# Two diffusion layers on one core: the experts' results go through a table in DRAM, and their weights through 16 fixed homes of half a unit

## The chip, the core and the metric

The kernel runs on one core of a Trainium2 chip. The metric is the device time of one execution in microseconds (us). A core has a matrix engine (TensorE, PE in the rows; PEld is its loading of weights), a vector engine (VectorE, DVE), a scalar engine (ScalarE, ACT), GpSimd (POOL) and SyncE (SP), which here only starts transfers. Each has its own queue of instructions, and they wait for each other by semaphores. 16 DMA engines move data between DRAM and the core's memory.

## The reference, cut to what matters

Two layers over 256 latent tokens of width 1024 with 256 context tokens, all in float32. The even layer mixes attention and a Fourier part and has a dense SwiGLU; the odd layer has a gated short convolution, and then eight experts of which each token uses two:

```
D_MODEL, SEQ, N_EXPERTS, TOP_K, D_EXPERT = 1024, 256, 8, 2, 3584

def swiglu(h, w_gate, w_up, w_down):
    return (jax.nn.silu(h @ w_gate) * (h @ w_up)) @ w_down

def moe_swiglu(h, router, w_gate, w_up, w_down):
    probs = jax.nn.softmax((h @ router).astype(jnp.float32), axis=-1)
    vals, idx = lax.top_k(probs, TOP_K)
    wts = vals / jnp.sum(vals, axis=-1, keepdims=True)
    combine = jnp.sum(jax.nn.one_hot(idx, N_EXPERTS, dtype=jnp.float32) * wts[..., None], axis=-2)
    out = jnp.zeros_like(h)
    for e in range(N_EXPERTS):
        out = out + combine[..., e:e + 1] * swiglu(h, w_gate[e], w_up[e], w_down[e])
    return out

# in reference(), second layer:
    x = x + gt1 * rmsnorm(y_lat, g_post_mix)
    h_lat = modulate(x, g_pre_ch, sh2, sc2)
    y_lat = moe_swiglu(h_lat, o_router[o], o_exp_gate[o], o_exp_up[o], o_exp_down[o])
    x = x + gt2 * rmsnorm(y_lat, g_post_ch)
```

## The kernel before

**Weights.** All large weights come as one stream of units of 128 x 4096 floats (2.1 MB). The first 54 units (`BASE`) belong to everything ahead of the experts; each expert has 21, namely 14 of gate and up columns (`GU_UNITS`) and 7 of down rows. SyncE loads each unit in two halves of 1.05 MB into a ring of 7 units (`RING`), in the order of the stream (line 275). A half is loaded into a slot when TensorE's products with the half that stood there are done: semaphores `first_used` and `used` go one way, `landed` the other. The sum `acc` (128 x 6144) and the gates' rows `gg` are buffers beside the ring. By the time of the experts much of `acc` is free.

**Ahead of the experts** come the modulation products, attention, the dense feed-forward (gate and up products line 1272, down products line 1235, the latter beginning at about 327 us), the convolution (line 1323) and the router. DVE picks two experts for each token, gives each token a slot in the lists of its experts, and chooses for each expert the smallest of seven widths (`WIDTHS`) that holds its list. GpSimd writes the normalized rows to a DRAM buffer (`rows_store`) and the lists to another (`slot_table`).

**An expert.** TensorE has an arm of code for each width and jumps into the arm of the next expert at the end of one (`enter_arm`). Widths 64 and 96 are narrow: the tokens stand still in TensorE and the weights stream (line 1511), 64 slots by two tiles of the array side by side and blocks of 32 slots by four; the products are then turned by transposes (`turn`, line 1470). The others are wide: the weights stand still (line 1486). ACT applies Silu (line 583) and DVE multiplies (line 985). The down products (`down`, line 1553) go into PSUM banks 4 to 7. In this run the eight experts have 64, 96, 144, 64, 128, 64, 96 and 64 slots; that is read from the forms of the instructions.

At the end of an expert the following happens in this order. ACT and DVE copy the down products to `y_slot` (lines 604 and 990), for which they wait on `ye_ps`; where a width has fewer than four parts, a semaphore instruction ahead of the last down unit (line 1532) counts up for the missing ones. TensorE turns the rows of the next expert, which GpSimd has fetched by the token list (line 380) into `xn`: 16 transposes, `turn_expert`, line 1413, after down unit `TURN_AFTER`, the last one. ACT and DVE scale and shift them into `hTe` (lines 558 and 931). Then TensorE multiplies `y_slot` by a weighted selection `selT`, which DVE makes in `weigh`, so that each token's row gets its share (`combine`, line 1583), and DVE adds the result to `y_sum` (line 996). After the last expert follow the norm and the output.

Of the kernel before, what the change touches and what calls it, by code (L numbers as in the profile page):

```python
# [21 lines left out]
P = 128  # L22
# [25 lines left out]
TURN_AFTER = NFE // 4 - 1  # L48
# [41 lines left out]
assert PER_EXPERT % RING == 0 and len(WIDTHS) <= 8  # L90
LAPS = PER_EXPERT // RING
HALF = UNIT // 2

# [12 lines left out]
def build(nc, stream, x_in, ctx_in, vecs, consts, rope, dft, gains, ada_b, norm_w, late, out):  # L106
    ctx = ExitStack()
    with ctx:
# [12 lines left out]
        acc = sb("acc", [P, 6 * D])  # L121
        gg = sb("gg", [P, 2, D])
# [11 lines left out]
        rows_store = nc.dram_tensor("rows_store", (SEQ, D), F32).ap()  # L134
        slot_table = nc.dram_tensor("slot_table", (SEQ * E, 2), F32).ap()
# [35 lines left out]
        y_sum = acc[:, 0:2048].rearrange("p (b d) -> p b d", b=TB)  # L171
        y_slot = acc[:, 2048:4096].rearrange("p (b d) -> p b d", b=2)
        empties = aT[:, 5632:5664]
        sel = acc[:, 4096:4608].rearrange("p (b s) -> p b s", b=TB)
        slot_list = acc[:, 4608:4704].rearrange("p (c w) -> p c w", w=2)
        entry = acc[:, 4704:4712].rearrange("p (b j w) -> p b j w", b=TB, w=2)
        selT = acc[:, 5120:5632].rearrange("p (b t) -> p b t", b=2)
        ramp, before, beats = acc[:, 5632:5889], acc[:, 5889:6017], acc[:, 4720:4848]
        iota, iota1 = ramp[:, 0:SEQ], ramp[:, 1:SEQ + 1]
        duel = acc[:, 2048:2304].rearrange("p (b e h f) -> p b e h f", b=TB, e=E, h=2)  # L180
        router_s = acc[:, 4848:4912].rearrange("p (k e) -> p k e", e=E)
        shift_r = acc[:, 4912:4976].rearrange("p (e k) -> p e k", e=E)
        shift_sum, shift_logit = acc[:, 4976:4984], acc[:, 4984:4992]
        junk = hTe[:, :, :].rearrange("p k t -> p (k t)").rearrange("p (b d) -> p b d", b=TB)

        def small(a, n, w):
            return acc[:, 6024 + a:6024 + a + 2 * n].rearrange("p (b e) -> p b e", b=TB)[:, :, 0:w]
# [6 lines left out]
        first_used = [sem(f"first_used{s}") for s in range(RING)]  # L194
# [29 lines left out]
            sem(n) for n in ("router_ok", "shift_ps", "rows_free", "hTe_wide", "y_sq"))  # L224

# [10 lines left out]


# [31 lines left out]
        def _(sp):  # L269
# [13 lines left out]
            with sp.Fori(1, BASE // RING + 1) as lap:  # L283
                for s in range(RING):
                    sp.wait_ge(used[s], lap)
                    for h in range(2):
                        load(lap * RING + s, s, h)
            lap = BASE // RING + 1
            for s in range(RING):
                if (lap - 1) * RING + s < BASE:  # L290
                    sp.wait_ge(used[s], lap)
                else:
                    sp.wait_ge(first_used[s], 1)
                load(lap * RING + s, s, 0)
# [1438 lines left out]
```

## Time and profile before

| | |
|---|---|
| time, median of 3 runs | 1483.48 us (1483.24 to 1487.16) |
| the profiled execution | 1484.72 us |
| its span in the trace | 1482.8 us |
| TensorE busy | 1432.0 us (97%) |
| VectorE, ScalarE, GpSimd busy | 374.6, 252.4, 42.5 us |
| DMA | 477.09 MB, mean 322 GB/s |

The span runs from the first to the last instruction; the time has some 2 us more. Busy time of TensorE is counted with modelled ends of the matmuls, so that small waits between two can be hidden in it. In the chain of work a piece named "issue" is time in which the engine waited for nothing that the profile shows.

### The profile page before, as it was taken

The page shows a single profiled execution, that of the slowest core. Times are in us where ns is not written, and L with a number is a line of the kernel's source. Part 1 is how long each engine was busy: PE and PEld are TensorE (multiplying, and loading weights), DVE is VectorE, ACT ScalarE, POOL GpSimd, SP SyncE. Part 2 cuts the span into 40 slices and gives each one's busy share as a digit, 9 for nine tenths or more (in the row PEclk, how much of TensorE's full clock was granted, in tenths as well). Part 3 has the DMA queues.
Part 4 walks back from the last instruction along what each step waited for, and adds up shares of the span by engine and source line. Part 5 has one row for each costly group of instructions (what it writes and reads, how often), then busy time and mean ns, then how long its engine had stood idle before and what let it go on. Part 6 is the DMA issues. An engine that isn't in the chain of part 4 may idle for free.

```text
span 1482.8 us, 22551 instructions
## 1 busy us (share of the span) xinstructions
PE 1432.0 (97%) x9386; PEld 921.0 (62%) x9386; DVE 374.6 (25%) x654; ACT 252.4 (17%) x517; POOL 42.5 (3%) x55
## 2 busy tenths in 40 slices
PE   6999999999999989999999999998999999999996
PEld 3456698874498566355379963555996464553452
DVE  3587533420156441111010000211010111110222
ACT  3154300001010132111010000221000122120221
POOL 1000010000000012000000000000000000000000
PEclk9999999999999989999999999999999999999998
DMA  9971576860769569999987776899988899999995
GB/s 376 383 294 59 222 314 236 324 235 4 272 238 354 207 201 415 421 419 421 421 356 264 261 261 234 333 421 419 420 309 308 291 419 421 419 420 421 415 421 242
DMA packets 69106, 477.09 MB, mean 322 GB/s; under 512 B 9491, under 2 KB 9827, under 8 KB 12176
## 3 DMA queue, kind: packets, MB, share of 16 engines
q1 hardware_dynamic: 64768, 467.92, 79.3%
q0 software_dynamic: 3952, 6.60, 1.3%
q8 instruction: 89, 1.46, 0.4%
q10 hardware_dynamic: 288, 1.05, 0.2%
q14 instruction: 9, 0.07, 0.0%
HBM read 478.73 MB, written 2.12 MB: 324 GB/s over the span
## 4 chain that ended last, share of the span: by engine, by line
PE 86%; DMA 7%; DVE 4%; SPq 2%; issue 1%; ACT 0%; DVEq 0%
PE ps L1511 24%; PE ps L1553 15%; PE ps L1486 14%; PE ps L1272 10%; DMA ring<-stream 7%; PE ps L1235 7%; PE ps L1323 6%; DVE acc L684 2%; PE ps L1583 2%; PE ps L1470 2%; SPq L275 1%; PE ps L1246 1%; PE ps L1153 1%; PE ps L1413 1%; PE ps L1115 1%
## 5 line engine op out<-in xcount | busy, mean ns | idle before, releaser
L1511 PE MATMUL ps<-ring,hTe 128*64 128x256 f32 (+1 forms) x3584 | 359.3, 383 | 4.7 <-issue 4.7
L1511 PEld LDWEIGHTS ps<-ring,hTe 128*64 128x64 f32 (+1 forms) x3584 | 215.1, 130 | 126.4 <-issue 17.5
L1553 PE MATMUL ps<-ring,aT 128*64 128x512 f32 (+2 forms) x1232 | 286.4, 597 | 5.4 <-DMA ring<-stream 4.0
L1486 PE MATMUL ps<-hTe,ring 128*128 128x144 f32 (+1 forms) x1792 | 212.0, 282 | 7.0 <-issue 7.0
L1486 PEld LDWEIGHTS ps<-hTe,ring 128*128 128x128 f32 x1792 | 211.6, 192 | 8.6 <-issue 8.6
L1553 PEld LDWEIGHTS ps<-ring,aT 128*64 128x64 f32 (+2 forms) x1232 | 96.6, 139 | 184.9 <-issue 172.1
L985 DVE TENSOR_TENSOR aT<-hT,ps 128x512 f32<-128x512 f32 x112 | 77.0, 688 | 517.0 <-ACT hT L583 517.0
L1272 PE MATMUL ps<-hT,ring 128*128 128x256 f32 (+1 forms) x832 | 153.5, 347 | 0.4 <-issue 0.4
L583 ACT ACTIVATE hT<-ps 128x512 f32<-128x512 f32 x112 | 66.9, 597 | 509.0 <-PE ps L1511 303.9
L1272 PEld LDWEIGHTS ps<-hT,ring 128*128 128x128 f32 x832 | 138.0, 191 | 16.5 <-issue 1.7
L684 DVE SCALAR_TENSOR_TENSOR acc<-ring,silu_c,acc 128x1024 f32<-128x1024 f32 x80 | 102.7, 1284 | 7.3 <-DMA ring<-stream 4.4
L1235 PE MATMUL ps<-ring,aT 128*128 128x512 f32 x208 | 90.7, 594 | 0.0
L1323 PE MATMUL ps<-hT,ring 128*128 128x256 f32 (+1 forms) x480 | 84.0, 338 | 0.4 <-issue 0.4
L1323 PEld LDWEIGHTS ps<-hT,ring 128*128 128x128 f32 x480 | 76.2, 191 | 8.6 <-issue 1.2
L990 DVE COPY acc<-ps 128x512 f32<-128x512 f32 x16 | 10.7, 689 | 241.5 <-PEq L1532 218.8
L1235 PEld LDWEIGHTS ps<-ring,aT 128*128 128x128 f32 x208 | 39.1, 190 | 49.0 <-issue 49.0
L604 ACT ACTIVATE acc<-ps 128x512 f32<-128x512 f32 x16 | 9.6, 598 | 259.8 <-PE ps L1553 157.9
L576 ACT ACTIVATE aT<-ps 128x512 f32<-128x512 f32 x84 | 49.8, 593 | 18.2 <-PE ps L1470 18.2
L1054 PE MATMUL ps<-ring,hT 128*128 128x512 f32 x96 | 42.1, 593 | 1.1 <-DVE hT L660 1.1
L1470 PEld LDWEIGHTS ps<-cst,aT 128*128 128x128 f32 x98 | 12.5, 139 | 35.2 <-issue 35.2
L380 POOL DMA_INDIRECT xn<-rows_store,token_at x14 | 14.1, 1004 | 675.0 <-PE ps L1413 587.2
L1054 PEld LDWEIGHTS ps<-ring,hT 128*128 128x128 f32 x96 | 18.0, 190 | 22.7 <-issue 22.0
(217 smaller groups left out, 711.1 us busy)
## 6 DMA issues: line engine op xcount, KB each, us to landing
ring<-stream SPq DMA_DIRECT2D x444, 1024.0 KB, 13.7
gg<-norm_w POOLq DMA_DIRECT2D x4, 512.0 KB, 9.1
x<-x_in SPq DMA_DIRECT2D x1, 1024.0 KB, 5.1
hTe<-ctx_in SPq DMA_DIRECT2D x1, 1024.0 KB, 21.0
rows_store<-xn POOLq DMA_DIRECT2D x1, 1024.0 KB, 5.3
out<-x ACTq DMA_DIRECT2D x2, 512.0 KB, 2.6
aT<-dft POOLq DMA_DIRECT2D x1, 512.0 KB, 8.3
aT<-rope POOLq DMA_DIRECT2D x1, 256.0 KB, 6.7
```

The costliest lines, as they stand in the source:

```text
L576: act.activation(aT_e[:, u, :, :].rearrange("p b n -> p (b n)"), ps[:, 6 + u % 2, :], ACT.Copy).then_inc(eT_ok, 1)
L583: act.activation(gated_e[:, u % 2, :, :], ps[:, q:q + 2, 0:SEQ], ACT.Silu).then_inc(e_silu, 1)
L684: last = dve.scalar_tensor_tensor(out=dst, in0=slot(what)[:, k * D:(k + 1) * D][:, cols], scalar=silu_c[:, 4 * h + k, 0:1], in1=dst, op0=A ...
L985: dve.tensor_tensor(aT_e[:, u, :, :], gated_e[:, u % 2, :, :], ps[:, q:q + 2, SEQ:2 * SEQ], ALU.mult).then_inc(e_a, 1)
L1054: last = pe.matmul(ps[:, blk, :], lhs[:, k, b * P:(b + 1) * P], w[:, k, :], start=(k == 0), stop=(k == KD - 1))
L1235: last = pe.matmul(ps[:, 4 + 2 * b + h, :], lhs(k)[:, b * P:(b + 1) * P], w[:, k % per_unit, h * BANK:(h + 1) * BANK], start=(k == 0), sto ...
L1272: last = pe.matmul(ps[:, j % 4, g * SEQ + t0:g * SEQ + t1], w[:, j % 2, g, k, :], hT[:, k, t0:t1], start=(k == 0), stop=(k == KD - 1))
L1323: last = pe.matmul(ps[:, bank, c + t0:c + t1], w[:, i % 4, k, :], hT[:, k, t0:t1], start=(k == 0), stop=(k == KD - 1))
L1470: last = pe.transpose(ps[:, 6 + u % 2, b * 256 + c * P:b * 256 + (c + 1) * P], aT_e[:, u, b, c * P:(c + 1) * P], ident)
L1486: last = pe.matmul(ps[:, 2 * (u % 2) + b, g * SEQ:g * SEQ + width], w, hTe[:, k, 0:width], start=(k == 0), stop=(k == KD - 1))
L1511: last = pe.matmul(to, hTe[:, k, s0:s0 + n], w, start=(k == 0), stop=(k == KD - 1))
L1553: last = pe.matmul(ps[n * r:n * (r + 1), 4 + bank, :], a_T, w[:, f, half * BANK:(half + 1) * BANK], start=(j < max(1, tiles // 2)), stop=( ...
```

## The change

A narrow or wide expert's result no longer goes through a product and a sum in `acc`. For all experts but the last, ACT writes `y_slot` (`store_from`, which picks the width's `store_blocks` by nested branches) to a new DRAM table `y_store` with a row for each slot and expert (8.4 MB). GpSimd fills the table with zeros once, early in the kernel. In the last expert GpSimd fetches for each token the row of its first expert (into `y_sum`, which is now `xn`) and later the row of its second (into `y_more`, which is `hTe`), and DVE weighs and adds them. A token's row in the last expert is still zero in the table; that expert's result is combined by TensorE as before. `weigh` and `combine` run once, and `combine` is a body of code beside the arm (`last_name`).

The next expert's rows are turned after down unit 3 in place of the last. In the down products, blocks of 32 slots use four tiles of 256 columns each for every row block, in place of two of 512 columns whose partial sums the combining product joined.

The experts' weights lie in 16 fixed homes of half a unit: the 14 halves of the ring, one at columns 0 to 2047 of `acc`, and one at columns 5120 to 7167 of the joined buffer `acc` and `gg`. The list `HOME` says where each of the 42 halves of an expert goes; it is the same for every expert, since an arm's code is. A half waits for the half that had its home before. Some small tables in `acc` move for this, and `y_sum` needs no zeros at the start.

```
-TURN_AFTER = NFE // 4 - 1
+TURN_AFTER = 3
...
+HALVES = 2 * PER_EXPERT
+HOME = [0, 1, 2, 3, 4, 5, 6, 7, 8, 9, 10, 11, 12, 13, 14, 15,
+        1, 0, 3, 4, 5, 6, 2, 9, 11, 8, 12, 13,
+        1, 0, 3, 4, 14, 5, 6, 7, 9, 10, 11, 12, 13, 15]
+STAYS = [HOME.count(h) for h in range(HOMES)]
+STAY = [HOME[:p].count(HOME[p]) for p in range(HALVES)]
+RETURNED = 96
...
+        def home_at(home):
+            if home >= 2 * RING:
+                at = (0, 5 * D)[home - 2 * RING]
+                return wide_acc[:, at:at + HALF]
+            return ring[:, ring_slot(home), home % 2 * HALF:(home % 2 + 1) * HALF]
@@ SyncE @@
+            with sp.Fori(1, E) as e:
+                for p in range(HALVES):
+                    home = HOME[p]
+                    if home == LAST_HOME:
+                        if STAY[p]:
+                            sp.wait_ge(given_back[home], e * (STAYS[home] - 1) + STAY[p])
+                        else:
+                            sp.wait_ge(ye_ps, e * 4)
+                    else:
+                        sp.wait_ge(given_back[home], e * STAYS[home] + STAY[p])
+                    load_half(e, p)
@@ GpSimd @@
+            pool.wait_ge(gu_ps, NF)
+            pool.dma_start(y_store.rearrange("(p r) d -> p r d", p=P),
+                           zeros.unsqueeze(1).to_broadcast([P, SEQ * E // P, D])).then_inc(y_zero, 16)
...
+            def fetch_results(dst, j, back):
+                for b in range(TB):
+                    pool.indirect_dma_start(
+                        out=dst[:, b, :], out_offset=None, in_=y_store,
+                        in_offset=bass.IndirectOffsetOnAxis(ap=row_at[:, 2 * b + j:2 * b + j + 1], axis=0),
+                    ).then_inc(back, 16)
+            pool.wait_ge(gather_ps, 4 * E)
+            pool.wait_ge(returned, RETURNED * E)
+            fetch_results(y_sum, 0, y_back)
+            pool.wait_ge(e_ps, E * GU_UNITS)
+            fetch_results(y_more, 1, y_more_back)
@@ ScalarE, end of an expert @@
+                with act.If(e < E - 1):
+                    take_gather(e * 4 + 4)
+                act.wait_ge(returned, e * RETURNED + RETURNED)
                 for b in (1, 0):
                     act.wait_ge(ye_ps, e * 4 + 4 - 2 * b)
                     act.activation(y_slot[:, b, 0:BANK], ps[:, 4 + 2 * b, :], ACT.Copy).then_inc(ye_act, 1)
+                def store_blocks(blocks):
+                    act.wait_ge(ye_act, e * 2 + 4)
+                    act.wait_ge(ye_dve, e * 2 + 4)
+                    count = 0
+                    for b, (s0, n) in enumerate(blocks):
+                        cols = D // (P // n)
+                        for r in range(P // n):
+                            act.dma_start(by_slot[s0:s0 + n, e, r * cols:(r + 1) * cols],
+                                          y_slot[n * r:n * (r + 1), b, 0:cols]).then_inc(returned, 16)
+                            count += 16
+                    if count < RETURNED:
+                        act.sem_inc(returned, RETURNED - count)
                 with act.If(e < E - 1):
-                    take_gather(e * 4 + 4)
+                    store_from(0)
@@ VectorE, last expert only @@
+                with dve.Else():
+                    weigh()
+                    dve.wait_ge(y_back, 16 * TB)
+                    for b in range(TB):
+                        last = dve.tensor_scalar(y_sum[:, b, :], y_sum[:, b, :], rt[:, 6, b:b + 1], None, ALU.mult)
+                    link(last)
+                    dve.wait_ge(y_more_back, 16 * TB)
+                    for b in range(TB):
+                        last = dve.scalar_tensor_tensor(out=y_sum[:, b, :], in0=y_more[:, b, :],
+                                                        scalar=rt[:, 7, b:b + 1], in1=y_sum[:, b, :],
+                                                        op0=ALU.mult, op1=ALU.add)
@@ TensorE @@
                     if u == 1:
-                        pe.wait_ge(comb_ok, e * 4 + 4)
+                        pe.wait_ge(ye_act, e * 2 + 2)
+                        pe.wait_ge(ye_dve, e * 2 + 2)
@@ down @@
-                                for half in (h,) if tiles == 1 else (0, 1):
-                                    r = half * (tiles // 2) + f % (tiles // 2) if tiles > 1 else 0
-                                    last = pe.matmul(ps[n * r:n * (r + 1), 4 + bank, :], a_T,
-                                                     w[:, f, half * BANK:(half + 1) * BANK],
+                            for part in parts:
+                                r = 0 if tiles == 1 else part
+                                last = pe.matmul(ps[n * r:n * (r + 1), 4 + 2 * b + h, 0:cols], a_T,
+                                                 w[:, part * cols:(part + 1) * cols], start=(j == 0), stop=(j == NFE - 1))
@@ arm @@
                     down(e, width)
-                    combine(e, width)
                     pe.reg_alu(at, at, 1, ALU.add)
-                    pe.br_lt(at, E, on_true=f"after{width}", on_false="experts_done")
+                    pe.br_lt(at, E, on_true=f"after{width}", on_false=f"last{width}")
```

## Rows read from the trace of the kernel before

**Rows 1.** Page, part 2: GB/s moved in 40 slices of 37 us.
```profile
GB/s 376 383 294 59 222 314 236 324 235 4 272 238 354 207 201 415 421 419 421 421 356 264 261 261 234 333 421 419 420 309 308 291 419 421 419 420 421 415 421 242
```

**Rows 2.** Busy us by stretch (PE, PEld, DVE, ACT, POOL), then clock, DMA share, GB/s.
```profile
543.00:629.00 86.00, 83.54 (x603) 43.12 (x604) 16.66 (x39) 19.72 (x35) 14.68 (x24) 1.00 0.97 386
...
1178.00:1261.00 83.00, 82.47 (x601) 43.50 (x603) 14.54 (x25) 19.72 (x35) 1.04 (x2) 1.00 0.99 404
1261.00:1388.00 127.00, 123.33 (x1175) 60.89 (x1173) 17.89 (x29) 19.70 (x35) 0.93 (x1) 1.00 1.01 420
1388.00:1470.00 82.00, 80.33 (x574) 41.41 (x572) 11.66 (x18) 16.32 (x30) 0.00 (x0) 0.98 0.94 390
```

**Rows 3.** Chain of work in order of time: start us, us, what.
```profile
543.10 7.06 PE ps L1511 x64
...
626.83 1.92 PE ps L1583 x8
...
749.17 3.63 PE ps L1583 x16
752.80 3.15 issue
...
929.82 5.35 PE ps L1583 x16
...
1018.55 3.81 issue
...
1174.12 3.44 PE ps L1583 x8
...
1467.61 1.96 PE ps L1553 x8
```

**Rows 4.** Timeline of TensorE at the experts' ends: start, us, instruction, idle before.
```profile
622.99 1.94 PE L1553 MATMUL ps<-ring,aT 128*64 128x512 f32 x8 [0.46 <-DMA ring<-stream]
...
935.87 4.32 PE L1511 MATMUL ps<-ring,hTe 128*64 128x256 f32 x38 [0.70 <-issue]
...
1022.37 0.82 PE L1486 MATMUL ps<-hTe,ring 128*128 128x128 f32 x5 [3.81 <-issue]
...
1178.53 7.13 PE L1511 MATMUL ps<-ring,hTe 128*64 128x256 f32 x64 [0.97 <-issue]
...
1256.91 1.97 PE L1413 MATMUL ps<-cst,xn 128*128 128x128 f32 x16
```

**Rows 5.** Timeline of ScalarE at the ends of e3, e4 and e5.
```profile
1014.78 0.60 ACT L604 ACTIVATE acc<-ps 128x512 f32<-128x512 f32 x1 [3.80 <-PE ps L1553]
...
1157.83 0.60 ACT L604 ACTIVATE acc<-ps 128x512 f32<-128x512 f32 x1 [32.88 <-PEq L1532]
1172.41 0.60 ACT L604 ACTIVATE acc<-ps 128x512 f32<-128x512 f32 x1 [13.99 <-PE ps L1553]
...
1259.56 1.28 ACT L583 ACT_TABLE_LOAD   x1
```

**Rows 6.** Groups by form from 543 us on: tiles of 32 slots.
```profile
L1511 PE MATMUL ps<-ring,hTe 128*32 128x256 f32 x896 | 51.2, 380 | 0.0
...
L1553 PE MATMUL ps<-ring,aT 128*32 128x512 f32 x336 | 39.8, 597 | 1.4 <-ACT aT L576 1.4
```

**Rows 7.** Busy us, clock, DMA share and GB/s behind the fifth expert.
```profile
1178.00:1182.00 4.00, 3.47 (x32) 2.43 (x34) 0.36 (x1) 0.00 (x0) 0.00 (x0) 1.00 0.55 214
...
1186.00:1464.00 278.00, 274.33 (x2264) 139.78 (x2262) 41.75 (x67) 53.84 (x97) 1.98 (x2) 0.99 1.01 419
```

**Rows 8.** DMA queues from 1178 to 1470 us: packets, MB, share.
```profile
q1 hardware_dynamic: 16208, 117.97, 97.6%
q0 software_dynamic: 576, 0.53, 0.5%
```

**Rows 9.** Time to landing of 1 MB from GpSimd's queue (line 346).
```profile
DMA to landing us min/median/max: 5.3/5.3/5.3
```

**Rows 10.** ScalarE's issues of transfers (line 615), duration in ns.
```profile
L615 ACTq DMA_DIRECT2D out<-x x2: 338/364/391, 1477.1 to 1479.8; - x2
```

More of the change, by code:

```diff
@@ L282, in _ @@
                     load(s, s, h)
[L283 removed]
+            with sp.Fori(1, BASE // RING) as lap:
                 for s in range(RING):
@@ new lines, in _ @@
+            with sp.Fori(1, E) as e:
+                for p in range(HALVES):
+                    home = HOME[p]
+                    if home == LAST_HOME:
+                        if STAY[p]:
+                            sp.wait_ge(given_back[home], e * (STAYS[home] - 1) + STAY[p])
[4 more added lines that the diff above has]
+                    load_half(e, p)
@@ L1534, in down @@
                               for h in (((1, 0) if d == final else (0, 1)) if n == P else (0,))]
-                    first_pass, last_pass = passes[0], passes[-1]
-                    for b, (s0, n) in (blocks[::-1] if d == final else blocks):
+                    for b, h in passes:
+                        s0, n = BLOCKS[width][b]
                         tiles = P // n
+                        parts = [h] if tiles == 1 else range(tiles)
+                        cols = D // max(tiles, 2)
                         if d == 0 and b == 1 and not is_wide(width):
@@ L1563, in down @@
-                        if d < final and b == len(blocks) - 1:
-                            last.then_inc(used[s], 1)
+                        for f in range(4):
+                            if f == 2 and (b, h) == passes[0]:
+                                landed_of(e, GU_UNITS + d, 1)
+                            j = 4 * d + f
+                            w = half_at(GU_UNITS + d, f // 2)[:, f % 2 * D:(f % 2 + 1) * D]
+                            u = j // 2 if tiles < 4 else 2 * d + 1
+                            c = n * (f % 2 if tiles < 4 else f)
+                            a_T = aT_e[:, u, b, c:c + n]
+                            if is_wide(width):
+                                a_T = aT_e[:, j // 2, j % 2, s0:s0 + n]
+                            for part in parts:
+                                r = 0 if tiles == 1 else part
+                                last = pe.matmul(ps[n * r:n * (r + 1), 4 + 2 * b + h, 0:cols], a_T,
+                                                 w[:, part * cols:(part + 1) * cols], start=(j == 0), stop=(j == NFE - 1))
+                                if count < len(done):
+                                    half_done(last, done[count], 1)
+                                elif f == 2 and (b, h) == passes[-1] and part == parts[0]:
+                                    half_done(last, GU_UNITS + d, 0)
+                                count += 1
@@ L1565, in down @@
+                        if d == final:
+                            last.then_inc(ye_ps, 2 if (b, width) == (1, 96) else 1)
+                        elif (b, h) == passes[-1]:
+                            half_done(last, GU_UNITS + d, 1)
                         if d == 0 and b == 0 and not is_wide(width):
```

235 lines of the change are left out of this document (133 added, 102 removed).

## The prediction, made before the changed kernel was run

> **What bounds the kernel now.** I read the rate row of the profile's page first, then the busy time by stretch, the chain of work in order of time, the waits and timelines at the ends of the experts, and last the DMA answer for the end of the run. The eight experts fill the span from 543.1 us to about 1470 us, and in it TensorE is hardly ever idle: 83.5 of 86 us, 82.5 of 83, 123.3 of 127 and 80.3 of 82 in the four stretches shown [rows 2]. So TensorE sets the time. But the DMA engines stand right behind it. They carry 420 GB/s whenever they are full [rows 1, 2], and one expert is 42 half units of 1.049 MB, so 42 x 2.5 = 105 us. An expert on 64 slots (the first, fourth, sixth and eighth; I call them e0, e3, e5, e7) takes TensorE 78.4 us: from 1178.5 to 1256.9 in e5 [rows 4]. Such an expert eats 10 or 11 halves of the stock in the ring. One on 96 slots (e1, e6) takes about 120 us and gives 6 back; the two on 144 and 128 slots (e2, e4) fill the ring, and the rate falls there to some 250 to 350 GB/s [rows 1]. After e4 come 64, 96 and 64 slots, and the DMA runs full for 278 us without a break [rows 7]. In e7 TensorE is idle 1.7 us in all [rows 2]: stock and demand run out nearly together. That is what the reader should keep in mind: before the end of e4 a saved microsecond of TensorE counts, after it only one of the DMA does.
>
> **The change part by part.** F is the end of e4's last down product, the start of the first instruction of the next expert's turn, 1172.4. The last eight matmuls of e7 start at 1467.6 [rows 3], F + 295.2.
>
> *Combining products.* Seven of eight go. Up to F four count: 1.92 (e0), 3.63 (e1), 5.35 (e2) and again 1.92 (e3, same kind as e0's), together 12.8 us [rows 3]. DVE's additions behind them were hidden. The three after F (3.44, 1.92, 3.63) stand in the part that the DMA will set.
>
> *The turn of the next expert's rows* (16 transposes, 1.9 us [rows 4]) is moved from after the last down unit to after unit 3; all seven stay. It needs rows that GpSimd fetched an expert earlier. For the sum only this counts: e4's now lies ahead of F, +1.75 us.
>
> *The jump to the next arm.* Idle times called "issue" follow the combining products: 3.15 and 3.81 us ahead of the wide arms [rows 3], 0.70 and 0.97 after wide ones [rows 4]. No data is missing, hTe is long there. In e3 the combining products could be issued when ACT's copy ended, 1014.78 + 0.60 = 1015.4, they are 8 and fit the queue, and the next arm starts at 1022.4 [rows 4, 5]: the jump costs about 6.9 us from issue. It is covered by what is already queued. ACT saw the semaphore that stands ahead of the final unit at 1157.8 [rows 5], while that unit's 16 matmuls, at 0.43 us each before 1172.4, began at 1165.5. So some 16 to 18 matmuls are queued ahead. Without combining products the jump is issued 16 matmuls before F: 6.9 us ahead in a wide expert (its gap goes), 3.4 us in a narrow one (a gap of 6.9 - 3.4 = 3.5 stays). Up to F: 3.15 to 3.5, 0.70 to 0, 3.81 to 3.5, so -0.7 us. Bounds: 0 if the queue covers all (-7.7), 6.9 everywhere (+13 for e1, e2, e3). From arm 64 to arm 96 there is no gap now, the code lies next to it.
> The Trainium skill (Runtime: NRT & Kernel Launch, Instruction fetch mechanics) says that a taken branch out of the two-page window stalls until a DMA has fetched the page. By it alone, with nothing queued, all far jumps would cost 6.9 us; the trace agrees on the kind of the gap and differs in that the queue hides part.
>
> *Tiles of 32 slots.* The 32-slot block now has 32 matmuls of 256 columns in place of 16 of 512. The nearest rows: 39.8 us / 336 = 118 ns and, for 256 columns in the same tile form, 51.2 / 896 = 57 ns [rows 6]. 16 x 118 = 1.9 against 32 x 57 = 1.8 us a unit: nothing. Bounds -0.6 to +0.6 us an expert.
>
> *Homes.* A ring of 14 gives way to 16 fixed ones; since 42 is no multiple of 16, ten homes are used three times an expert and six twice, and a half waits for the one that stood 12 to 28 places before it. Reading HOME backwards from the first halves of an expert (distances 13, 15, 20 and more, 15, 15, 14, ...) all of 0 to 12 may be in place when the last unit of the expert before runs; 13, 14, 15 are asked for within 2 us of its end. In the middle the distance falls to 12, but on 64 slots half 28 is due at about 38 us and its home is free at 33, so the queue isn't held up. In e0 it works thus: the start finds 15 halves landed in place of 14, the last half, which TensorE now gets at 622.99 after a wait [rows 4], comes 3.7 us sooner (two halves less, 5.0, but the 16th is asked for only at 543.1, and half 16 only when half 1 is used, 1.3). e0 took 624.9 - 543.1 = 81.8 us, 3.4 more than e5's 78.4 [rows 3, 4]; that stall goes. But e1 then starts with one or two halves in place and takes three in its first 6 us: I estimate waits of 2.3 us. Net -1.1.
>
> Up to F: -12.8 - 0.7 - 1.1 + 1.75 = -12.85, so F' = 1159.5.
>
> *From F' to the last load.* Before, the turn, 3.44 of products and 0.97 of jump gave the DMA 6.1 us in which it ran out of free places (214 GB/s from 1178 to 1182 [rows 7]); it was full again about F + 10, with 112 halves to come (117.97 MB on the ring's queue [rows 8]). After, it is full from about F' + 1, since three halves are asked for at once, with 113 to come: -9 + 2.5 = -6.5 us. Into the same stretch fall the new transfers: results of e4, e5, e6 by ACT's queue (128, 64, 96 rows of 4 KB: 0.52 + 0.26 + 0.39 MB) and GpSimd's four fetches of 128 rows for the last sum (2.10 MB). 3.3 MB at 420 GB/s are 7.8 us. All lie ahead of the last weights: the second fetch starts at the end of e7's gate and up products. Together +1.3: the last eight matmuls start at F' + 296.5 = 1456.0, against 1467.6: -11.6 us.
> TensorE by itself would be there at F' + 295.2 - 9.0 (three combining products) - 0.97 - 1.75 - 1.7 (idle time in e7) = F' + 281.8. So 14 to 15 us of waits for loads open up after F', most in e7.
> Bounds of the 7.8: at least the bytes at full rate, so it can't be less; at most, by 5.3 us from issue to landing of 1 MB alone [rows 9] for each of 3.3 MB, 17.5. I take 7.8, since the small queue's 0.53 MB took 0.5% against 97.6% for 118 MB [rows 8], nearly the same price by the byte. The Trainium skill (DMA: Bandwidth & Descriptors, Bandwidth) gives 6.15 us for 1 MB from GpSimd: by that the fetches alone would cost 12.3 in place of 5 and the gain would be 4.3 us.
>
> *Hidden.* 8.4 MB of zeros go out from about 327 us. The DMA stands at 4 GB/s in the slice 333 to 370 [rows 1]; at 420 GB/s it takes 20 us, at 1 MB in 5.3 us [rows 9] 42, to 371: covered; were it twice that, loads for the convolution would be late by up to 10 us. ACT's stores: 2 to 6 issues of 0.36 us [rows 10] after its copy, then a table load of 1.28 us [rows 5]; Silu is needed by TensorE 7 us after the arm starts. DVE's weighting in e7 (four operations, some 4 us) waits for fetches issued 25 us before the end. The tail after the last down product is as before.
>
> Sum: the profiled execution took 1484.7 us for a span of 1482.8. 1484.7 - 11.6 = 1473.1. The median of the runs shown is 1.2 below the profiled one, so 1471.9.
>
> **The rivals.**
> 1. *TensorE still sets the end.* If the loads kept pace, all savings count: the last eight start at 1159.5 + 281.8 = 1441.3, 26 us sooner, about 1457. For it: only 1.7 us of idle time in e7 now. Against: 14 us would have to come from a DMA that is at its limit for 278 us [rows 7]. 0.12.
> 2. *The new transfers cost more than their bytes*, at most the 17.5 us above in place of 7.8: 9.7 us more, 1481.6; half of that, or the lead of one home lost (2.5), 1474 to 1477. The queue's shares [rows 8] speak against the full price. 0.13. The Trainium skill's 6.15 us (above) would be a case of this, at 1479.
> 3. *Slower: ScalarE's code.* The loop body of ACT grows by six arms of stores. Today the table load of the next expert follows the last Identity at once [rows 5], so its loop has no page to fetch. If its jumps (into a store arm, and back) each cost 6.9 us like TensorE's, Silu comes 13.8 us late. Counting the copy, two stores, the table load, Silu and DVE's product, the first unit's result would stand 4.1 us after F and then 17.9; TensorE asks for it 7.1 us after F on 64 slots, 10.8 on 96, and 18 on the wide ones: 10.8 us of waits in e3 and 7.1 in e1, 17.9 against 11.6 saved, with up to 2.3 back since e1 then no longer waits for loads: 1488 to 1490. It turns the sign where the delay D at each end makes 2D - 9.7 more than 11.6, from 10.7 us on. 0.07.
> 4. *No gain:* the jumps cost their 6.9 us uncovered at e1, e2, e3 (+13, the upper bound above): 1485. Against: the queue ahead shown in [rows 5]. 0.06.
> My forecast: 0.62.
>
> **How the numbers follow.** 1471.9 is the likeliest; its own range is 1467 to 1477 (2.3 of waits in e1 or none, 0.6 by the tiles, the lead of a full two homes for -2, the 7.8 up to 11). The range for 8 in 10 goes to 1460 and 1481 and leaves out most of rival 1 and the worse parts of 3 and 4. 0.3% of 1483.5, 4.4 us, is what this kernel's runs can tell from no change. Faster by more: forecast, rival 1 and most of 2, 0.84. Within: 0.09. Slower: 0.07.
>
> **What would show it.** Right: TensorE's start of e5 12 to 14 us sooner, less so at the end; no idle time at the jumps out of the wide experts, 3 to 4 us out of narrow ones; the window from e5 on at full rate without the dip to 214 GB/s; waits for loads of 12 to 15 us in e7. Wrong: e7 without them (rival 1); a last load more than 299 us after F' (rival 2); TensorE waiting for ACT's Silu in the third unit of e3 (3); gaps of 6 us and more at each jump (4); a rate above 4 GB/s past 380 us that isn't the ring's (the zeros).

## The result, and the profile of the changed kernel

The changed kernel takes 1474.57 us (median of 4 runs, 1472.15 to 1475.38), the kernel before beside it 1485.12 us (4 runs, 1483.24 to 1487.16): a ratio of 0.993, with a 95% interval from 0.9916 to 0.9944. So it is faster, by 10.6 us; 11.6 was the forecast, with 1471.9. The profiled execution took 1473.88 us for a span of 1471.9; 1473.1 was the forecast for it. Of the 2.7 us between the forecast and the measured median 0.8 are in the profiled execution; the rest is the step from it to the median, for which the prediction took 1.2 off, while here the median is 0.7 above.

I read the same views as before the change, in the same order. First the page, the rate row and the queues of the whole run:

```profile
GB/s 374 372 302 59 221 309 258 302 229 270 235 236 360 233 235 400 420 420 420 420 411 240 253 300 234 376 421 419 421 319 310 370 421 419 420 420 421 419 420 240
...
q1 hardware_dynamic: 64768, 467.92, 79.3%
q0 software_dynamic: 6592, 17.08, 3.1%
q10 hardware_dynamic: 1952, 3.80, 0.7%
```

The tenth slice, 270 GB/s where 4 stood [rows 1], holds the 8.4 MB of zeros. In the experts' part the pattern is that of [rows 1]: full rate in the narrow experts, less while e2 and e4 run, full rate from there to the end.

The chain of work in order of time (start, us, what) around the jumps and at the starts of the experts:

```profile
748.72 111.69 PE ps L1613 x896
...
1005.05 4.08 issue
1009.13 101.82 PE ps L1613 x896
...
1160.77 7.06 PE ps L1638 x64
...
1367.33 8.78 PE ps L1638 x64
```

1160.77 is F', the start of e5, right behind e4's last down product. Before, that product ended at F = 1172.4, so 11.6 us are saved up to there. (The first product of e5 itself stood at 1178.53 before [rows 4], behind the turn, the combining and the jump; by that mark it is 17.8 us.) The jump from e3 to e4 still shows as 4.08 us of "issue" (3.81 before [rows 3]).

The timeline of TensorE (start, us, instruction, idle time before it and what ended it) at the ends of e0, e2, e6 and e7:

```profile
621.41 1.89 PE L1681 MATMUL ps<-acc,aT 128*64 128x512 f32 x8
623.13 3.62 PE L1638 MATMUL ps<-ring,hTe 128*64 128x256 f32 x32
627.24 1.95 PE L1638 MATMUL ps<-ring,hTe 128*64 128x256 f32 x16 [0.49 <-DMA ring<-stream]
630.03 3.16 PE L1638 MATMUL ps<-ring,hTe 128*64 128x256 f32 x36 [0.84 <-DMA ring<-stream]
...
922.40 1.88 PE L1681 MATMUL ps<-acc,aT 128*128 128x512 f32 x4
924.21 7.13 PE L1638 MATMUL ps<-ring,hTe 128*64 128x256 f32 x64
931.72 0.33 PE L1596 MATMUL ps<-cst,aT 128*128 128x128 f32 x1 [0.38 <-DVE aT L1085]
...
1362.46 1.89 PE L1681 MATMUL ps<-acc,aT 128*64 128x512 f32 x8
1367.33 8.78 PE L1638 MATMUL ps<-ring,hTe 128*64 128x256 f32 x64 [2.98 <-issue]
...
1430.51 1.94 PE L1681 MATMUL ps<-ring,aT 128*64 128x512 f32 x8 [1.68 <-DMA ring<-stream]
1434.26 1.94 PE L1681 MATMUL ps<-acc,aT 128*64 128x512 f32 x8 [1.81 <-DMA acc<-stream]
...
1456.69 1.94 PE L1681 MATMUL ps<-acc,aT 128*64 128x512 f32 x8 [0.43 <-DMA acc<-stream]
```

Read it as four statements. The five waits of 0.27 to 0.65 us at the end of e0 (the last of them in [rows 4]) are gone and come back in part as two waits in e1. The arm of e3 starts with no gap behind a wide one, where 0.70 stood [rows 4]. Out of a narrow one there is a gap of 2.98. And in the down products of e7 TensorE waits for every half from the third on, 8.8 us in all: the last eight matmuls start at 1456.69, F' + 295.9.

ScalarE's timeline at the start of e3:

```profile
925.28 2.88 ACTq L685 DMA_DIRECT2D y_store<-acc  x5
929.05 1.28 ACT L652 ACT_TABLE_LOAD   x1 [4.14 <-issue]
```

Five store issues take 2.88 us, and the table load of the next Silu follows 0.9 us after them. Silu is then late by so little that TensorE waits 0.38 us (the line at 931.72 above). In the profile of `no_fetch` (experiment 1), with the same stores, no wait shows there.

Busy time, granted clock, DMA share and GB/s by stretch behind F', and in the last expert:

```profile
1161.00:1165.00 4.00, 4.00 (x40) 2.70 (x38) 0.00 (x0) 2.27 (x3) 0.00 (x0) 1.00 0.98 324
1165.00:1170.00 5.00, 5.00 (x47) 3.07 (x43) 1.38 (x2) 1.11 (x3) 0.00 (x0) 1.00 0.99 387
1170.00:1456.00 286.00, 271.85 (x2344) 139.49 (x2340) 39.97 (x60) 53.71 (x96) 5.78 (x6) 0.99 1.00 417
1364.00:1459.00 95.00, 82.87 (x576) 40.61 (x574) 15.61 (x22) 18.14 (x32) 3.79 (x4) 0.98 0.95 395
```

The dip to 214 GB/s [rows 7] is gone, and the DMA carries 417 GB/s up to the end. TensorE is idle for 14.15 of the 286 us, where it was idle for 3.7 of 278 [rows 7]. Of the 14.15, 2.98 are the jump into e7, which before had 2.98 too; the timeline shows 8.8 as waits for loads in e7 and 2.1 as waits for loads at the start of e6. The queues from 1161 to 1459 us (packets, MB, share of the 16 engines), and for three kinds of transfer their size and the median time to landing:

```profile
q1 hardware_dynamic: 16273, 118.50, 95.9%
q0 software_dynamic: 864, 2.31, 2.0%
q10 hardware_dynamic: 656, 1.18, 1.0%
...
y_store<-acc ACTq DMA_DIRECT2D x4, 128.0 KB, 7.3
...
xn<-y_store,row_at POOLq DMA_INDIRECT x2, 10.4
hTe<-y_store,row_at POOLq DMA_INDIRECT x2, 9.7
```

A fetch of 0.5 MB lands 10 us after its issue, but it moves among the loads and its share is that of its bytes: q0 and q10 together carry 3.5 MB in 3.0% of the time, q1 carries 118.5 MB in 95.9%.

### The profile page after: what moved, and what is told of

Its sections match the earlier page's. It is cut to its first block, busy times and chain, and to the rows that moved or that the text cites. A ratio compares the mean times of both kernels' runs of the same rounds, so it can differ in the third digit from the quotient of the medians.

```text
span 1471.9 us, 23068 instructions
## 1 busy us (share of the span) xinstructions
PE 1414.4 (96%) x9642; PEld 923.4 (63%) x9642; DVE 354.6 (24%) x612; ACT 253.0 (17%) x517; POOL 48.5 (3%) x61
## 4 chain that ended last, share of the span: by engine, by line
PE 83%; DMA 8%; DVE 4%; SPq 3%; issue 1%; ACT 0%; ACTq 0%; DVEq 0%
PE ps L1638 22%; PE ps L1681 15%; PE ps L1613 15%; PE ps L1387 10%; PE ps L1350 7%; DMA ring<-stream 6%; PE ps L1438 6%; DMA acc<-stream 2%; DVE acc L782 2%; PE ps L1596 2%; SPq L307 1%; PE ps L1361 1%; SPq L327 1%; PE ps L1268 1%; PE ps L1230 1%
## 5 line engine op out<-in xcount | busy, mean ns | idle before, releaser
L1638 PE MATMUL ps<-ring,hTe 128*64 128x256 f32 (+1 forms) x3328 | 338.3, 383 | 6.4 <-DMA ring<-stream 3.5
L1638 PEld LDWEIGHTS ps<-ring,hTe 128*64 128x64 f32 (+1 forms) x3328 | 200.6, 130 | 123.0 <-issue 15.4
L1681 PE MATMUL ps<-ring,aT 128*64 128x512 f32 (+2 forms) x1344 | 249.8, 505 | 7.9 <-DMA ring<-stream 6.5
L1613 PE MATMUL ps<-hTe,ring 128*128 128x144 f32 (+1 forms) x1664 | 198.9, 283 | 7.4 <-issue 7.4
L1613 PEld LDWEIGHTS ps<-hTe,ring 128*128 128x128 f32 x1664 | 198.3, 194 | 9.1 <-issue 9.1
L1681 PEld LDWEIGHTS ps<-ring,aT 128*64 128x64 f32 (+2 forms) x1344 | 91.5, 133 | 149.6 <-issue 123.0
L1027 DVE TENSOR_SCALAR hTe<-ps,ab 128x256 f32<-128x256 f32 x28 | 13.3, 538 | 153.8 <-PE ps L1528 153.8
L1681 PE MATMUL ps<-acc,aT 128*64 128x512 f32 (+2 forms) x224 | 44.3, 504 | 2.2 <-DMA acc<-stream 2.2
L623 ACT ACTIVATE hTe<-ps,ab 128x256 f32<-128x256 f32 x28 | 13.5, 564 | 132.1 <-PE ps L1528 132.1
L432 POOL DMA_INDIRECT xn<-rows_store,token_at x14 | 14.1, 1007 | 649.3 <-PE ps L1528 646.4
## 6 DMA issues: line engine op xcount, KB each, us to landing
y_store<-aT POOLq DMA_DIRECT2D x1, 8192.0 KB, 28.4
```

The costliest lines, as they stand in the source:

```text
L1613: last = pe.matmul(ps[:, 2 * (u % 2) + b, g * SEQ:g * SEQ + width], w, hTe[:, k, 0:width], start=(k == 0), stop=(k == KD - 1))
L1638: last = pe.matmul(to, hTe[:, k, s0:s0 + n], w, start=(k == 0), stop=(k == KD - 1))
L1681: last = pe.matmul(ps[n * r:n * (r + 1), 4 + 2 * b + h, 0:cols], a_T, w[:, part * cols:(part + 1) * cols], start=(j == 0), stop=(j == NFE ...
```

## The experiments

In each, "start of e5" and "last eight" are read from the timeline of TensorE of its profiled execution or from the chain of work (the two give the start of e5 0.07 us apart); after has 1160.77 and F' + 295.9. Medians are of the runs named; each ratio is to runs of the kernel before on the same chip. The experiments ran on three chips, and the medians of the kernel before beside them and beside the result go from 1483.65 to 1485.12 us: a difference between a median and that of after is uncertain by about 1.5 us.

**1. Is the price behind F' that of the bytes?** First the four fetches of GpSimd are cut to 16 columns, without their index (so the last sum is made of other data):

```
-                    pool.indirect_dma_start(
-                        out=dst[:, b, :], out_offset=None, in_=y_store,
-                        in_offset=bass.IndirectOffsetOnAxis(ap=row_at[:, 2 * b + j:2 * b + j + 1], axis=0),
-                    ).then_inc(back, 16)
+                    pool.dma_start(dst[:, b, 0:16], y_store[b * P:(b + 1) * P, 0:16]).then_inc(back, 16)
```

> The changed kernel, with GpSimd's four fetches of 128 rows of 4 KB in the last expert cut to 64 bytes a row; the last sum is thus left out of the computation. Theory (from the end of e4 on the DMA's bytes set the end): F', the end of e4's down products, stays at 1160.8 us; the last eight matmuls of e7 start 5 us sooner (2.1 MB at 420 GB/s), 291 us after F' in place of 295.9; the time falls by 5 us to about 1469.5. Rival (the waits in e7 come from the plan of homes or a late semaphore, the fetches fill gaps): no change. Rival (fetches cost more than their bytes, 5.3 us per MB): 10 us sooner.

Measured: 1469.42 us (4 runs), ratio 0.99 [0.9882, 0.9918]. e5 starts at 1163.36, the last eight at 1454.43, F' + 291.1. The 2.10 MB cost 4.8 us, as 2.10 MB at 420 GB/s (5.0). F' itself was 2.6 us later than in the profile of after: its waits in e1 are longer by 0.8 us, its jump into e4 by the same, and e4's gate and up products take 102.91 us in place of 101.82, none of which the edit touches.

Then ScalarE's stores are cut to 16 columns as well (so the table stays nearly all zeros):

```
-                            act.dma_start(by_slot[s0:s0 + n, e, r * cols:(r + 1) * cols],
-                                          y_slot[n * r:n * (r + 1), b, 0:cols]).then_inc(returned, 16)
+                            act.dma_start(by_slot[s0:s0 + n, e, r * cols:r * cols + 16],
+                                          y_slot[n * r:n * (r + 1), b, 0:16]).then_inc(returned, 16)
```

> As before, and ACT's stores of the experts' results cut to 64 bytes a row as well; the results of seven experts are thus left out. Theory: 1.2 MB less after F' is 2.8 us more, so the last eight start about 288 us after F'; in e1 the waits for loads at its start shrink by 0.6 us. Time 8 us below the changed kernel, about 1466.5. TensorE still waits some 5 to 6 us for loads after F'. Rival (the stores cost nothing, they use gaps): as without the fetches alone.

Measured: 1464.06 us (4 runs), ratio 0.9864 [0.9845, 0.9882]. e5 starts at 1158.81. Its last eight, in the timeline, and its queues behind F':

```profile
1446.84 1.94 PE L1678 MATMUL ps<-acc,aT 128*64 128x512 f32 x8 [0.42 <-DMA acc<-stream]
...
q1 hardware_dynamic: 16273, 118.50, 98.4%
...
q0 software_dynamic: 416, 0.25, 0.3%
q10 hardware_dynamic: 656, 0.03, 0.2%
```

F' + 288.0. The same 118.50 MB of weights, the same number of packets on ScalarE's queue, and the last of them is used 7.9 us sooner after F'. The term of 7.8 us stood for just this. The median is 10.5 us below after's, since F' is 2.0 us sooner as well; most of that is the jump into e4, 2.37 us in place of 4.08 (see the last section). That TensorE still waits for the last half shows that the end is set by the loads even without the table's traffic.

**2. Half the bytes, the same instructions.** The table and what is stored to it are bfloat16, so the results of all experts but the last are rounded; the fetches bring bfloat16 rows, which DVE weighs and adds in float32. The core of it:

```
-        y_store = nc.dram_tensor("y_store", (SEQ * E, D), F32).ap()
+        y_store = nc.dram_tensor("y_store", (SEQ * E, D), BF16).ap()
...
+        y_half = acc[:, 2048:3072].bitcast(BF16).rearrange("p (b d) -> p b d", b=2)
...
+                def copy_y(dst):
+                    act.wait_ge(returned, e * RETURNED + RETURNED)
+                    for b in (1, 0):
+                        act.wait_ge(ye_ps, e * 4 + 4 - 2 * b)
+                        act.activation(dst[:, b, 0:BANK], ps[:, 4 + 2 * b, :], ACT.Copy).then_inc(ye_act, 1)
+                with act.If(e < E - 1):
+                    take_gather(e * 4 + 4)
+                    copy_y(y_half)
+                with act.Else():
+                    copy_y(y_slot)
```

> The table and what is stored to it and fetched from it are bfloat16, so the results of all experts but the last are rounded to bfloat16; the instructions of TensorE, the number of transfers and their places stay. The 3.3 MB that fall behind the end of e4's down product become 1.65 MB, the zeros early in the kernel 4.2 MB in place of 8.4. If bytes set the price of the new transfers, 3.9 us of the 7.8 come back and the start of e5 stays: last eight matmuls at F' + 292 (after: + 295.9), median about 1470.7 against 1474.6 of after, ratio to before about 0.990. If the price lay in the number of transfers or of descriptors, nothing changes: F' + 296, 1474.6. If the end is set by TensorE, nothing either. A transfer of 4 KB rows that becomes one of 2 KB rows could also cost more by the byte: then between the two.

Measured: 1468.92 us (4 runs), ratio 0.9893 [0.9877, 0.991]: the fastest version here that still computes the whole result, at the price of that rounding. e5 starts at 1159.49; the last eight and the queues from 1155 to 1452 us:

```profile
1451.53 1.94 PE L1695 MATMUL ps<-acc,aT 128*64 128x512 f32 x8 [0.42 <-DMA acc<-stream]
...
q0 software_dynamic: 608, 1.26, 1.1%
q10 hardware_dynamic: 656, 0.59, 0.6%
```

F' + 292.0. The stores are as many as before (656 packets on q10 in both), and half of all the new bytes gives back half of the 7.8. So the bytes set the price, not the number of transfers; for the stores not that of packets either, since in experiment 1 their 3.1 us (F' + 291.1 to 288.0) went with the bytes at the same 656 packets. The four fetches are as many transfers as before too, but their packets fell with their bytes (864 packets on q0 behind F' in after, 608 here), so for them packets and bytes are not told apart.

**3. The homes.** All of the change but the homes, in number and in order: halves go round 14 places, as in the old ring.

```
-HOME = [0, 1, 2, 3, 4, 5, 6, 7, 8, 9, 10, 11, 12, 13, 14, 15,
-        1, 0, 3, 4, 5, 6, 2, 9, 11, 8, 12, 13,
-        1, 0, 3, 4, 14, 5, 6, 7, 9, 10, 11, 12, 13, 15]
+HOME = [p % 14 for p in range(42)]
```

> The changed kernel with the 42 halves of an expert put round robin into 14 homes, the halves of the old ring; the other two stay unused. Nothing of the computation changes. Theory: two homes are worth 3.7 us at e0, where the stall now comes back or moves to e1's start, so F' comes 3 to 3.7 us later, and 3 us behind F' (two halves less in stock, but one of the 16 was only asked for at the end of e4): together 6 to 7 us, 1481. Rival (all of the gain is TensorE's combining work, the homes are idle places): no change, 1474.6. Rival (the homes carry all of it): back to 1485.

Measured: 1483.22 us (10 runs), ratio 0.9994 [0.9983, 1.0006], no gain in the total. e5 starts at 1168.23, 7.5 us later than in after, the last eight at 1467.00, F' + 298.8. The part behind F' came as expected; the part ahead of it was twice what I had put. The timeline of TensorE shows where, at the ends of e0 and of e3:

```profile
622.80 1.94 PE L1679 MATMUL ps<-ring,aT 128*64 128x512 f32 x8 [0.76 <-DMA ring<-stream]
...
631.17 1.95 PE L1636 MATMUL ps<-ring,hTe 128*64 128x256 f32 x16 [1.23 <-DMA ring<-stream]
634.34 5.54 PE L1636 MATMUL ps<-ring,hTe 128*64 128x256 f32 x80 [1.22 <-DMA ring<-stream]
...
1006.66 1.94 PE L1679 MATMUL ps<-ring,aT 128*64 128x512 f32 x8 [0.98 <-DMA ring<-stream]
1009.14 1.94 PE L1679 MATMUL ps<-ring,aT 128*64 128x512 f32 x8 [0.55 <-DMA ring<-stream]
1015.89 19.33 PE L1611 MATMUL ps<-hTe,ring 128*128 128x128 f32 x151 [4.81 <-issue]
```

The block of 80 matmuls in e1 begins at 634.34. In the kernel before, the same 128 matmuls of e1 began at 628.68 and ran 10.72 us without a wait; the last 80 take 5.54, so that point lay at 633.9. With 14 places the combining product dropped in e0 brings nothing: the loads had been full since 543 us, and TensorE only reaches the wait sooner. The same happens in e3, where 1.53 us of waits stand in place of 0.30. With the 16 homes the block begins at 630.03, and e3's waits are gone. That total of nothing has parts that are not nothing. The combining products dropped in e1 and e2 do count: with 14 places e2 starts at 752.94, 3.0 us sooner than before, e3 at 928.43 against 935.87, and e4's last down product ends at 1168.23, 4.2 us ahead of F. Behind it 3.6 are lost (298.8 against 295.2), for there the table's 7.8 us of bytes come in and the dip at the start of e5 goes. So without the homes the combining products of e0 and e3 bring nothing and the rest pays just the table's traffic: TensorE's saved time needs a stock to live on where the loads are full. Whether the two more homes or their order do it was not separated. The homes alone, with the combining left in, were not tried, because their place is where `acc` held the sum. A seventeenth home, from which I expected another 4 us, does not fit: the core's memory has 3.9 KB a partition left, and half a unit takes 8.

**4. More work for TensorE, ahead of F' and behind it.** If the loads alone set the end behind F', 10.3 us more of TensorE's work in e6 must vanish, and 10.3 us in e1 or e4 must show in full. Three extra passes of the first block over the down unit 0 (their products are thrown away) in the arm that runs e1 and e6:

```
+                    if d == 0 and width == 96:
+                        landed_of(e, GU_UNITS, 1)
...
+                        for again in range(3):
+                            for f in range(4):
...
+                                for r in range(tiles):
+                                    pe.matmul(ps[n * r:n * (r + 1), 4, 0:BANK], a_T, w[:, r * BANK:(r + 1) * BANK],
+                                              start=(f == 0), stop=(f == 3))
```

> The changed kernel, in which the arm for 96 slots makes the products of the first block of down unit 0 three times more before it makes them in earnest; the result is the same. That is 48 matmul instructions or 10.3 us of TensorE in e1 and again in e6. Theory (TensorE sets the end up to the end of e4, the DMA's bytes after it): the 10.3 us of e1 count in full, e5 starts at about 1171; the 10.3 us of e6 vanish, since TensorE then waits that much less for loads in e7, and the last eight matmuls stay at 296 us after F'. Time 10 us above the changed kernel, 1485. Rival (TensorE sets the end throughout): 20.6 us more, 1495.

Measured: 1487.39 us (9 runs), ratio 1.0021 [1.001, 1.0031]; e5 starts at 1172.52, the last eight at 1468.93, F' + 296.4. Twice 10.3 us were added, and the profiled execution is 12.2 us longer than after's (the median 12.8). The passes in e6 cost 0.5 us at most. F' is 11.75 us later, 1.5 more than the passes in e1; 1.3 us more are in e4's gate and up products (103.10 us against 101.82), which the edit doesn't touch.

The same passes in the arm of 128 slots, which runs e4 only (`width == 128`):

> The changed kernel, in which the arm for 128 slots makes half of the products of down unit 0 three times more first; the result is the same. 24 instructions, 10.3 us of TensorE, in e4 alone. Theory: the homes are full there and the DMA stands still for lack of places, so nothing can make up for it: 10.3 us more, 1485, the last eight 296 us after F'. Rival (the loads set the pace in the whole stretch of experts, as the kernel with 14 homes might say, and a delay of TensorE anywhere is partly filled): 0 to 5 us more.

Measured: 1484.89 us (10 runs), ratio 1.0006 [0.9996, 1.0015], 10.3 above after; the last eight at 1468.47, F' + 295.7. Of the 12 us that e5 starts later in this profile, 1.5 were there when e2 began, ahead of the edit (750.18 against 748.72).

**5. What the jump costs.** TensorE waits, ahead of the jump, until ACT and DVE have copied the last down products, so nothing is queued when it jumps:

```
                     pe.reg_alu(at, at, 1, ALU.add)
+                    pe.wait_ge(ye_act, e * 2 + 4)
+                    pe.wait_ge(ye_dve, e * 2 + 4)
```

> The changed kernel, with TensorE's queue made to wait, ahead of each jump to the next arm, until ACT and DVE have copied the down products; nothing of the computation changes. Theory (a far jump costs 6 to 6.9 us from its issue, and what hides part of it is what is queued ahead): the jump is issued 0.7 us after the last product in place of 16 matmuls before it. Gaps of 7.6 us after e1 and e3 (3.3 and 4.1 now) and of 6 to 7.6 after e2 (none now), 0.8 after e0 which the wait for loads there takes in: 13 to 15 us more up to the end of e4's products; later gaps vanish in the waits for loads. 1487 to 1490. Rival (the gaps are a fixed price of the arm entered): 0.7 us at each of three ends, 1477.

Measured: 1501.20 us (4 runs), ratio 1.0116 [1.0099, 1.0132]. That is 26.6 us above after, far more than expected. The gaps are what the theory says, 7.71, 8.39, 7.88, 8.40 and 7.12 us; less the 0.60 us of the copy, the jump costs 6.5 to 7.8 us from issue at each of the five places, behind wide arms too, where after has no gap. The two jumps from the arm of 64 to that of 96, whose code lies next to it (e0 to e1, e5 to e6), have the same wait ahead of them and leave TensorE idle for 1.65 us only. A far jump thus costs 5.5 to 6.8 us more than a near one. Two things were missing in the expectation. Here is the end of e4 in the timeline, and the windows around it (busy time, granted clock, DMA share, GB/s):

```profile
1179.48 1.88 PE L1681 MATMUL ps<-acc,aT 128*128 128x512 f32 x4
1189.76 8.85 PE L1638 MATMUL ps<-ring,hTe 128*64 128x256 f32 x64 [8.40 <-issue]
```

```profile
1181.00:1184.00 3.00, 0.36 (x1) 0.00 (x0) 0.00 (x0) 1.14 (x2) 0.00 (x0) 1.00 0.78 229
1184.00:1190.00 6.00, 0.24 (x2) 0.24 (x4) 0.00 (x0) 0.74 (x1) 0.00 (x0) 0.71 1.00 378
1190.00:1195.00 5.00, 5.00 (x34) 2.92 (x34) 0.00 (x0) 0.00 (x0) 0.00 (x0) 0.67 0.38 153
1195.00:1200.00 5.00, 5.00 (x47) 3.11 (x45) 1.38 (x2) 1.68 (x3) 0.00 (x0) 1.00 0.64 221
```

First, the 64 matmuls behind the gap take 8.85 us in place of 7.13 (the same view of after): the granted clock is 0.67 over the first 5 us (full is 2.4 GHz, half is 1.2), after 8.4 us in which TensorE had done nothing. The gaps themselves add 16.6 us up to e4, and the end of e4 comes 20.6 us later; most of the rest is this, 2.5 us at the start of e3 (9.65 us for the same 64) and 1.3 in e2 (112.97 against 111.69). Second, I had held the gap behind e4 to be free, as all savings and losses behind F' are hidden by the loads. They are only while the loads run. When e4 ends, all homes but a few are full; the DMA fills the last ones, then falls to 153 GB/s until TensorE gives halves back. The last eight come at 1483.95, with the end of e4's down product at 1181.4 that is 302.5 later, 6.6 more than in after.

**6. The place of the turn.** The next expert's rows are turned after the last down unit again, all else as in after:

```
-TURN_AFTER = 3
+TURN_AFTER = NFE // 4 - 1
```

> The changed kernel with the turn of the next expert's rows after the last down unit again; nothing of the computation changes. Theory: behind a wide expert the jump and the scaling of hTe are no longer under down products: e3 starts 5 to 7 us after the end of e2's products in place of 0 (1.8 of it the turn itself), e2 and e4 about 7 us after the products in place of 3.3 and 4.1 plus the 1.9 of the turn ahead: up to the end of e4 some 7.5 us more, less 1.75 for e4's own turn, which then falls into the part that the loads set. 5 to 6 us more, 1480. Rival (the moved turn is only a transfer of 1.9 us from one place to another): no change.

Measured: 1478.94 us (7 runs), ratio 0.9968 [0.9956, 0.9979], 4.4 above after. At the start of e3 in the timeline:

```profile
923.11 1.91 PE L1528 MATMUL ps<-cst,xn 128*128 128x128 f32 x16
926.90 7.13 PE L1638 MATMUL ps<-ring,hTe 128*64 128x256 f32 x64 [1.88 <-issue]
934.85 0.33 PE L1596 MATMUL ps<-cst,aT 128*128 128x128 f32 x1 [0.82 <-DVE aT L1085]
```

The rows have to be scaled into `hTe` before the arm can start, now that no combining product stands between: 1.9 us of transposes and 1.88 of waiting, where after has nothing, and Silu is late by 0.82. I had expected 5 to 7 us at this place and it was 3.8. Out of narrow arms the gap is 4.98 in place of 3.31 and 4.08. The 16 transposes cost the same wherever they stand; the early turn takes their wait away, and without it 4.4 of the 10.6 us are lost (5.3 by the two ratios, each to the kernel before on its own chip).

## Why the prediction was right, step by step

**Up to F'.** The forecast was 1159.5, the profile has 1160.8: 11.6 us saved, a little less than the "12 to 14" that was named as a sign. The combining products are gone, their 12.8 us with them. Jumps: 3.5, 0 and 3.5 us were predicted for the starts of e2, e3 and e4, and 3.31, 0 and 4.08 came; the queue ahead hides a jump out of a wide arm and half of one out of a narrow arm, and experiment 5 shows the whole of it. The Trainium skill (Runtime: NRT & Kernel Launch, Instruction fetch mechanics) says that a taken branch to code outside the two pages held stalls for a fetch. The five gaps of 7.12 to 8.40 us agree with it, as do the 1.65 us at the two near jumps; that a fetch of code is what fills them, no row shows directly. The gap of 0 behind wide arms shows what the page leaves out, the work already queued. Of e0 and e1: the stall of 3.4 us went, as predicted, and e1 waited 1.8 us (122.2 us from 623.2 to 745.4 against 120.4), not 2.3.

What the sum did not have is the clock. e2's first five us, in the windows of after and (by the same view) of before:

```profile
748.70:753.70 5.00, 4.98 (x27) 4.99 (x28) 0.00 (x0) 1.28 (x1) 0.00 (x0) 0.66 1.02 418
```

```profile
755.90:760.90 5.00, 4.95 (x40) 4.95 (x41) 0.00 (x0) 0.00 (x0) 0.00 (x0) 1.00 1.02 410
```

The gaps ahead are nearly the same, 3.31 and 3.15 us, yet behind the first the clock had fallen and behind the second it had not: 27 matmuls against 40. The arm's 896 matmuls take 111.69 us in place of 110.02, and in the traces of the eight variants 111.41 to 112.97. This +1.7, with +0.4 for the gaps and -0.5 for e1's waits, is 1.6; the miss was 1.3.

**Behind F'.** 296.5 was the forecast, 295.9 came. Each piece was confirmed by itself: the dip at the start of e5 gone (324 GB/s in place of 214), the DMA full from then on, the traffic of the table 7.8 us by bytes for 7.9 in experiment 1 and 3.9 of 3.9 in experiment 2. One sign came out smaller than named: the waits for loads, 12 to 15 us expected in e7, are 8.8 there and 10.9 with those at the start of e6. The last eight start 14.1 us later than the 281.8 that TensorE would need by itself, but that figure is an estimate, and the 3.2 us between are not accounted for. The Trainium skill (DMA: Bandwidth & Descriptors, Bandwidth) gives 6.15 us for 1 MB from GpSimd. By that the fetches would have cost 12.3 us; they cost 4.8. The page does not say what a transfer costs among others that fill the engines, and there the measurement decides.

**Hidden work.** The zeros are hidden: the DMA moves 423 GB/s from 340 to 350 us, 207 in the next ten and 2 from 360 to 370, and TensorE is busy 10.00 of 10 us in each of the three. They land 28.4 us after their issue, between the 20 and 42 of the prediction. The tiles of 32 slots cost nothing that the arms' times show. DVE's last two weighting operations start at 1435.07, 22 us ahead of the last eight matmuls.

**The rivals.** Rival 1, TensorE sets the end, falls by experiment 4: 10.3 us of work in e6 vanish. Rival 2, dearer transfers, falls by experiments 1 and 2. Rival 3, ScalarE's code, showed nothing of its kind: after the last store 0.8 to 1.25 us pass to the table load, not 7. What the stores do cost is their own issues, 2.9 us for five and 3.4 for six, where 0.36 us each had been put, and 0.38 us at TensorE. Rival 4, uncovered jumps, is what experiment 5 makes by hand.

**Where a step was mis-sized.** Not in the sum, but in the share of its parts. I had given the homes a net 1.1 us ahead of F', a stall of 3.4 that goes less 2.3 of new waits, and 2.5 for one home's lead behind it; experiment 3 has 7.5 and 2.9. Of the four combining products of 12.8 us, taken as saved whatever the loads do, those of e0 and e3 (3.8 us) are saved only because the stock of 16 halves lets TensorE run ahead of the loads there; those of e1 and e2 count with 14 places too. The text said of the time ahead of F that a saved microsecond of TensorE counts there; in e0 and e3, with 14 places, it did not. And it held only the DMA's time to count behind F'. Experiment 5 agrees and shows the catch: a gap of TensorE that is long enough to fill the homes becomes time of the DMA, and 6.6 us were lost there.

## What to carry to other kernels

Where loads run at full rate through a stretch, time saved on the matrix engine in it is worth something only as far as buffers let the loads run ahead of the use; look for waits for loads at the end of each such stretch, and give a saving and a buffer together. Price new transfers in a stretch bound by DMA by their bytes at the rate of that stretch, not by their time to landing (10 us for 0.5 MB here, at a cost of 1.2). A far jump is best issued with as much work queued ahead as the queue holds, and a wait must not stand between that work and the jump.

## What the hardware showed that I had not expected

The granted clock can fall after a gap of 3 us and need not: behind 2.98 us in after e7's first 64 matmuls took 8.78 us, behind 2.89 in experiment 2 they took 7.25, and behind 3.15 in the kernel before e2 started at full clock. The length of the gap does not decide it: behind 2.90 us they took 8.81 in `no_traffic` (experiment 1) and 7.28 in `slow96` (experiment 4). Behind the gaps of 7.1 to 8.4 us in experiment 5 it fell at all three narrow arms that I looked at (8.85, 8.94 and 9.65 us). What decides in between I can't say from these runs.

A profile of the same code can differ by 2 to 3 us in the middle: F' was 1158.8, 1159.5, 1160.8 and 1163.4 in four kernels whose instructions ahead of it are nearly the same, by longer or shorter waits for loads in e1 and by jumps of 2.37 to 4.88 us into e4. Differences of that size were therefore read from F' on, or from the medians. But not all of it is chance: the jump into e4 takes 4.08 to 4.88 us in after and in the four profiles with the same stores and the same turn (`no_fetch`, `ring14`, `slow96`, `slow128`), and 2.62 and 2.37 in the two whose stores are halved or cut (experiments 2 and 1). So the stores' traffic seems to lengthen this jump by 1.5 us or more, a cost of the table ahead of F' that the prediction did not have; no run tests it by itself.
